# The long convolution's layer norm and its product, by halves of tokens

## What is computed

```python
def layernorm(x, g, b):
    mu = jnp.mean(xf, axis=-1, keepdims=True)
    var = jnp.mean(jnp.square(xf - mu), axis=-1, keepdims=True)
    y = (xf - mu) * lax.rsqrt(var + EPS)
    return (y * g + b).astype(x.dtype)

def conformer_conv(x, norm_g, pw1_w, pw1_b, dw_w, dw_b, ln_g, ln_b, pw2_w, pw2_b):
    a, b = jnp.split(rmsnorm(x, norm_g) @ pw1_w + pw1_b, 2, axis=-1)
    h = a * jax.nn.sigmoid(b)
    h = <causal convolution of width 31, each channel by itself>(h, dw_w) + dw_b
    h = jax.nn.silu(layernorm(h, ln_g, ln_b))
    return h @ pw2_w + pw2_b
...
        h = h + conformer_conv(h, ...)
        h = h + swiglu_ffn(h, ffn_norm[layer], ffn_w_in[layer], ffn_w_out[layer])
```

## Time and profile before

| | us |
|---|---|
| median of 3 runs | 1077.83 |
| lowest, highest | 1077.32, 1078.03 |
| the profiled execution, its own time | 1077.06 |
| its span in the trace | 1075.3 |
| TensorE busy | 1032.3 |
| VectorE busy | 700.5 |
| ScalarE busy | 531.0 |

### The profile page before, as it was taken

One profiled execution on the slowest core, in us unless ns is written; L12 is line 12 of the kernel. 1 busy time (PEld: TensorE's weight loads), 2 busy tenths in 40 slices (PEclk: granted clock), 3 DMA queues, 4 the chain that ended last, 5 costly groups with the idle time before them and its releaser, 6 DMA issues.

```text
span 1075.3 us, 15964 instructions
## 1 busy us (share of the span) xinstructions
PE 1032.3 (96%) x6529; PEld 888.0 (83%) x6529; DVE 700.5 (65%) x1085; ACT 531.0 (49%) x809; POOL 79.4 (7%) x125
## 2 busy tenths in 40 slices
PE   6997999999999989999999999999899999999997
PEld 6984788888889846888888889988678889998996
DVE  3997566666668587666766668848665456555554
ACT  5424455545554477654455464436465445434442
POOL 2000093000001011000000011000000000000000
PEclk9998999999999989999999999999999999999999
DMA  8873546667555501756676546644234435565530
GB/s 226 235 211 101 154 137 202 173 204 206 178 118 180 180 1 38 218 157 196 178 210 200 169 148 226 192 158 158 79 126 150 156 118 189 164 200 191 180 134 40
DMA packets 188995, 174.21 MB, mean 162 GB/s; under 512 B 12822, under 2 KB 164502, under 8 KB 188922
## 3 DMA queue, kind: packets, MB, share of 16 engines
q1 hardware_dynamic: 187216, 169.67, 51.8%
q10 hardware_dynamic: 1322, 2.62, 0.8%
q0 software_dynamic: 384, 0.90, 0.2%
HBM read 171.24 MB, written 1.93 MB: 161 GB/s over the span
## 4 chain that ended last, share of the span: by engine, by line
PE 79%; DVE 12%; ACT 4%; DMA 2%; issue 2%; POOL 0%; SPq 0%; POOLq 0%; ACTq 0%; DVEq 0%
PE bank L1866 17%; PE bank L1867 16%; PE bank L1868 16%; PE bank L1951 11%; PE bank L1950 6%; DVE split_lo L1115 4%; PE bank L2093 2%; ACT split_hi L675 2%; PE bank L1947 2%; DVE xn L1132 1%; DMA v<-in_ml_conv_w 1%; PE bank L2258 1%; PE bank L1903 1%; PE bank L1948 1%; DVE v L1572 1%
## 5 line engine op out<-in xcount | busy, mean ns | idle before, releaser
L1115 DVE TENSOR_TENSOR split_lo<-raw,split_hi 128x2048 fp32r<-128x2048 f32 (+1 forms) x157 | 354.6, 2273 | 146.3 <-ACT split_hi L675 145.9
L675 ACT ACTIVATE split_hi<-raw 128x2048 fp32r<-128x2048 f32 (+1 forms) x157 | 295.2, 1893 | 84.5 <-PE bank L1868 77.4
L1866 PE MATMUL bank<-xn,split_hi 128*128 128x256 f32 (+1 forms) x752 | 215.7, 287 | 5.3 <-DVE xn L1132 4.6
L1951 PE MATMUL bank<-xn,split_hi 128*128 128x512 f32 x616 | 219.8, 396 | 0.0
L1867 PE MATMUL bank<-xn,split_hi 128*128 128x256 f32 (+1 forms) x752 | 212.6, 283 | 0.0
L1868 PE MATMUL bank<-xn,split_lo 128*128 128x256 f32 (+1 forms) x752 | 212.5, 283 | 0.0
L1950 PE MATMUL bank<-xn,split_lo 128*128 128x256 f32 x616 | 172.2, 280 | 0.5 <-DVE xn L1132 0.5
L1866 PEld LDWEIGHTS bank<-xn,split_hi 128*128 128x128 f32 (+1 forms) x752 | 143.0, 190 | 10.4 <-issue 4.4
L1867 PEld LDWEIGHTS bank<-xn,split_hi 128*128 128x128 f32 (+1 forms) x752 | 143.1, 190 | 0.7
L1868 PEld LDWEIGHTS bank<-xn,split_lo 128*128 128x128 f32 (+1 forms) x752 | 143.1, 190 | 0.0
L1951 PEld LDWEIGHTS bank<-xn,split_hi 128*128 128x128 f32 x616 | 115.6, 188 | 23.7
(11 more groups left out here) (322 smaller groups left out, 1203.4 us busy)
## 6 DMA issues: line engine op xcount, KB each, us to landing
raw<-in_ffn_w_in SPq DMA_DIRECT2D x88, 512.0 KB, 5.2
raw<-in_w_ff SPq DMA_DIRECT2D x32, 1024.0 KB, 5.3
raw<-in_ffn_w_out SPq DMA_DIRECT2D x22, 1024.0 KB, 5.0
raw<-in_w_in SPq DMA_DIRECT2D x14, 1024.0 KB, 5.3
raw<-in_a_pw_w SPq DMA_DIRECT2D x16, 512.0 KB, 7.9
raw<-in_w_xkv SPq DMA_DIRECT2D x8, 1024.0 KB, 5.4
raw<-in_a_pw_w SPq DMA_DIRECT2D x4, 1024.0 KB, 9.0
raw<-in_b_w_in SPq DMA_DIRECT2D x4, 1024.0 KB, 6.0
```

Of the source, the lines that this page charges most:

```text
L675: nc.scalar.activation(split_slot[m % SPLITS][0][:, 0:n], raw[c % RAWS][:, 0:n], ACT.Copy).then_inc(split_hi, 1)
L1115: return nc.vector.tensor_tensor(dst, src, hi.bitcast(F32), ALU.subtract)
L1866: mm(dst, left[0], right[0], start=start, stop=False)
L1951: x = mm(whole, hi, xn_both[:, :, kt, :], start=False, stop=kt == KT - 1)
```

## The change

- The last convolved tile (7) is computed in two halves of tokens into two banks (5 and 6), evacuated and squared by halves. In place of five sums of tiles on TensorE there are one over a tile that VectorE has summed (tiles 0, 1, 5 and 6, in `tile_sum`) and two of 128 columns for tile 7; in place of four sums of squares there are one for tile 4 (before the last convolution), one over what VectorE has summed, and two of 128 columns for tile 7. So "last tiles in a row" are tile 7's halves, and the order of squaring becomes tiles 2 to 4, 0 and 1, 5 and 6, 7.
- The square of the offset goes to ScalarE. The load of the Sqrt table goes ahead of the evacuation of tile 5.
- Reciprocal, centring, normalising, SiLU and splitting are done for the first 128 tokens of all tiles and then for the other 128. ScalarE makes the high part (`ACT.Copy`); VectorE only the low one.
- The first column half of the product runs over token halves outside and channel halves inside, so it holds two chunks at a time.
- The bias row is no product any more: it is loaded over all 128 partitions (512 KB in place of 4) and added to `h` by VectorE, in two instructions of 128x1024 between the last SiLU tile and the split of `pw2[2]`.

```diff
-        SQUARES = [slice(2, 5), slice(5, 7), slice(0, 2), slice(7, 8)]
+        SQUARES = [slice(2, 5), slice(0, 2), slice(5, 7), slice(7, 8)]
+        tile_sum = softf[:, 0:S]
+        LAST_BANK = [5, 6]
+        NORMED = [[1, 2, 3, 3, 4, 4, 5, 5], [6, 6, 7, 7, 8, 8, 9, 9]]
...
-                sc.dma_start(pw2_row, a["a_pw2_b"]).then_inc(small_loaded, 16)
+                sc.dma_start(gain_row[:, :], a["a_pw2_b"].broadcast_to([P, D])).then_inc(bias_loaded, 16)
...
+            nc.scalar.activation(msq[:, 18:19], eps_col[:, :], ACT.Sqrt)
             conv_evac(3)
+            square_about_pivot(0)
             conv_evac(4)
-            square_about_pivot(0)
             square_about_pivot(1)
             square_about_pivot(2)
-            conv_evac(5)
-            square_about_pivot(3)
-            nc.scalar.activation(msq[:, 18:19], eps_col[:, :], ACT.Sqrt)
+            for t in range(TT):
+                sc.wait_ge(quad_done, 6 + t)
+                nc.scalar.activation(v[:, 7, tok(t)], bank[LAST_BANK[t]][:, tok(t)], ACT.Identity,
+                                     bias=vecT[:, col["a_dw_b"] + 7:col["a_dw_b"] + 8]).then_inc(conv_out, 1)
+            for t in range(TT):
+                sc.wait_ge(centred, 4 + t)
+                part = u[:, 7, PAD + P * t:PAD + P * t + P]
+                nc.scalar.activation(part, part, ACT.Square).then_inc(squared, 1)
+            sc.wait_ge(offset_ready, 1)
+            nc.scalar.activation(offset, offset, ACT.Square).then_inc(offset_squared, 1)
...
+            for t in range(TT):
+                for ft in range(KT):
...
+                    sc.wait_ge(normed, NORMED[t][ft])
+                    nc.scalar.activation(v[:, ft, tok(t)], v[:, ft, tok(t)], ACT.Silu,
...
+                    if first or ft % 2:
+                        part = (slice(None), slice(ft if first else ft - 1, ft + 1), tok(t))
+                        sc.wait_ge(silu_ready, n + 1)
+                        nc.scalar.activation(xn[0][part], v[part], ACT.Copy).then_inc(silu_hi, 1)
...
             for g in range(4):
-                silu_halves(g)
+                silu_low(g, 0)
                 if g + 2 < 4:
-                    centre(g + 2)
-                    normalise(g + 2)
+                    centre(g + 2, 0)
+                    normalise(g + 2, 0)
+                if g == 2:
+                    inverse(1)
+                    centre(0, 1)
+                    normalise(0, 1)
+            centre(1, 1)
+            normalise(1, 1)
+            for g in range(4):
+                silu_low(g, 1)
+                if g + 2 < 4:
+                    centre(g + 2, 1)
+                    normalise(g + 2, 1)
+            ve.wait_ge(bias_loaded, 16)
+            for t in range(TT):
+                nc.vector.tensor_tensor(h[:, t, :], h[:, t, :], gain_row[:, :], ALU.add).then_inc(bias_added, 1)
             through(chunk_of["pw2"][2])
...
+                parts = [weights("pw2", 0, 4)]
+                for t in range(TT):
+                    for half in range(2):
...
+                        c, w = parts[half]
+                        for q in range(4):
+                            kt = 4 * half + q
+                            te.wait_ge(silu_lo, NORMED[t][kt])
+                            x = mm3(bank[acc_bank(FFN0, t, 0)][:, :], part(xn, ALL, kt, tok(t)), part(w, ALL, q, ALL),
+                                    kt == 0, kt == KT - 1)
```

190 lines of the change are left out of this document (110 added, 80 removed).

## The result

| | before | after |
|---|---|---|
| median of 4 runs each, on one chip | 1077.74 | 1070.76 |
| lowest, highest | 1077.32, 1078.03 | 1068.90, 1071.45 |
| the profiled execution, its own time | 1077.06 | 1068.90 |
| its span in the trace | 1075.3 | 1067.0 |

The ratio is 0.9934, with a 95% interval of 0.992 to 0.9947: the change makes the kernel 7.0 us faster, between 5.7 and 8.6 us. Repeated beside another set of runs it was 1071.87 against 1077.78, 5.9 us, a ratio of 0.9945 (0.9927 to 0.9963). The forecast was 1071.8 and the range 1069.2 to 1075.2. The first median lies just under the forecast's own part of that range (1070.8 to 1073.0), the second inside it.

A forecast was written before the change was run, and what follows sets the result against it. TensorE, 96% busy, bounds the kernel, its longest wait a 5.5 us chain ahead of `pw2`. Split of `pw2[2]` at 111.5 plus 12.0 gives 123.5 instead of 129.54: 1077.83 - 6.0 = 1071.8, range 1069.2 to 1075.2.

The forecast's parts named there:

- just there: Last convolution's start: its rows' last load has landed by 85.62, in time for a start at 85.75.
- The nearest row: Last convolution: measured 64-column pieces at 0.034 us each, taken for the 128 pieces of 128 columns, 4.35 us.
- a late convolution: Rival at the last convolution: late rows or pieces at 0.056 cost 2 us, giving 1073.8; chance 0.09.
- The statistics, the root and the first tile: Ahead of the product: variance closed at 92.95, 1.3 us sooner; first SiLU 95.0; first product 96.2 against 99.95.
- neither bound: Tiles' end, forecast 106.9: 104.9 if VectorE never waits, 108.5 if a 128-token SiLU costs as much as 256.
- The cover of 6.5 us: Split of `pw2[2]` before: ended 108.8, wanted 115.3; now forecast to end at 111.5, TensorE waiting 1.2 us.
- TensorE bound instead of the split: Rival in the product: tiles end at 104.9 or the clock stays up; gain 7.3 to 8.5 us, 1069.3 to 1070.8; chance 0.19.
- the second fall: Rival: the clock falls again behind the wait for `pw2[2]`, costing 1.7 to 3 us, 1073.5 to 1075; chance 0.12.
- a sign of being wrong: Wrong if the `pw2[2]` wait is missing or over 3 us, clock differs, or later stages aren't all 6 us earlier.
- a clock that stays low: Slower rival in the product: each us low costs 0.47, gain gone past 118.9, up to 1087 us; chance 0.04.
- The bias row's term: Four bias products of 1.05 us leave TensorE, three of them on the path: 3.2 us.
- given back: Rival behind the stretch: longer waits in the attention layers eat the gain, within 2 us of before; chance 0.06.

The follow-up runs named there:

- e9: The changed kernel with ScalarE issuing the bias row's broadcast load later, behind the squares of tiles 5 and 6; median 1070.84 us, ratio 0.9946 to the kernel before.
- e10: The changed kernel with the late bias row load and VectorE splitting `pw2[2]` before adding the bias row; median 1068.59 us, ratio 0.9928 to the kernel before.
- e12: The changed kernel with late load, nine unread products in TensorE's wait, and `pw2[2]` split ahead of tile 7's squares; 1068.10 us, ratio 0.9919 to before.
- e7: The changed kernel with nine additional unread products in TensorE's wait ahead of the product; median 1071.80 us, ratio 0.9943 to the kernel before.
- e8: The changed kernel with nine unread products in TensorE's wait and `pw2[2]` split before the bias row is added; 1068.89 us, ratio 0.9915 to before.
- e6: The changed kernel with VectorE splitting `pw2[2]` before it adds the bias row; median 1069.69 us, ratio 0.9930 to the kernel before.
- e5: The changed kernel run again unaltered, beside another set of runs; median 1071.87 us, ratio 0.9945 to the kernel before.
- e1: The kernel before with only the bias row loaded over all partitions and added by VectorE ahead of the `pw2[2]` split; 1073.00 us, ratio 0.9956.
- e11: The changed kernel with late load, `pw2[2]` split before the bias row, and nine unread products in TensorE's wait; 1068.88 us, ratio 0.9921 to before.

## Why the prediction was right

Its times lean on `conv(4)` ending at 85.3. In the changed kernel's trace that is 84.29, so 1.02 is added to each mark here.

| | predicted | measured + 1.02 |
|---|---|---|
| the last convolution starts | 85.75 | 86.64 |
| its pieces | 4.35 for 128 | 3.63 |
| the variance is closed | 92.95 | 93.20 |
| first SiLU | 95.0 | 95.17 |
| first product; the wait ahead of it | 96.2; 4.3 | 96.47; 4.18 |
| clock back | 102.1 | 101.6 |
| last low part | 106.9 | 107.1 |
| TensorE wants `pw2[2]` | 110.0 to 110.4 | 110.04 |
| its split ends | 111.5 | 111.57 |
| wait for it | 1.2 | 1.59 |
| the second half | 12.0 | 11.93 |
| the feed-forward network's first product | 123.5 | 123.56 |

**The last convolution** is where two terms were wrong and cancelled. Its rows were not "just there": it started 1.33 us behind the end of `conv(4)`, 0.70 of that in a wait, where the prediction had 0.45. With the load of the bias row later it is 0.57 in e9, but 0.73 in e10 and 0.70 in e12, and with the early load 0.72 and 0.70 in e7 and e8; so the load is a likely cause and not a shown one. Part of it belongs to the one sum, which took 0.57 and not 0.45 even without a wait. And the pieces of 128 columns did not cost 0.034 but 3.63 / 128 = 0.028. The nearest row, 64 columns at 0.034, was no guide: halving the width from 256 (0.056) halved the cost. Here the measurement goes with the Trainium skill ("TensorE: Matmul & The Clock Gate", section LDWEIGHTS): its rule, columns over 1.2 GHz, makes an estimate of 27 ns for the weight load of 32 columns, just under the 28 ns that a piece took. The prediction had set it aside for the row. Had both terms been right, the sum would have been nearly the same; that they cancelled is luck. The rival of a late convolution thus did occur, at 0.9 us instead of 2, and was paid for by the pieces.

**The statistics, the root and the first tile** came within 0.3 us. The table load was what came last, and the reciprocal of half the tokens took the 0.95 us estimated, the SiLU 0.49.

**The tiles.** ScalarE and VectorE take turns as worked out. In the second token half VectorE waits for ScalarE's copy by 0.27, 0.17 and 0.80 us, the last low part's start comes at 105.66, and neither bound (104.9, 108.5) was near.

**The bias row and the new wait.** VectorE needed 2.35 + 2.28 us behind the last low part, as the sum had it. The cover of 6.5 us was gone, and the split of `pw2[2]` became what TensorE waits for. e6 shows it as the cause. The wait is 0.4 longer than predicted, by the sum chiefly because the clock came back 0.8 us sooner behind the product's start (0.4 us at 0.47 each), which TensorE could use for nothing else: the rival "TensorE bound instead of the split" names the same thing, that an unfallen clock would only lengthen this wait, and e7 shows it (2.60 us) along with the second fall, at some 1.6 us. In the change itself the second fall did not come.

**The clock** took another course than forecast, which the prediction had named as a sign of being wrong. It was to fall about 1.2 us into the wait and be back 5.9 us after the product's start; it fell 2.5 us in and was back after 5.1, and in e5, the same kernel, it fell only 0.7 us after the product had begun and was back 4.1 us after its start. The time did not feel it, since VectorE's split set the end of the first half: the stretch is 36.92 and 36.91 us. Had TensorE been what bound, this would have been an error of 0.4 us in the one and 1.2 in the other. Two smaller readings were off: the low stretch behind 763 lasts 3.6 us in the trace of before (from 764.4 to 768.0) and not 3.2, and by the rival's own terms (6.0 and 1.2 us at 0.47 each) a clock that stays low eats the gain from about 117.5 on, not 118.9.

**The bias row's term** of 3.2 us on the path was too small, at 3.75 (e1). The forecast did not go by it: the 12.0 us of the second half were built from products, and are right.

**Behind the stretch** nothing was given back: the distance is 7.0 us at 129.54, 165.55, 316.54 and 340.54 of the trace before, and only the two falls of the clock in the attention layers add to it. By medians the gain is 7.0 and 5.9 us in two sets of runs, and 6.0 was the sum.

The first median, 1070.76, could as well be claimed by the rival "TensorE bound instead of the split" (1069.3 to 1070.8); it is the wait of 1.59 us and e6 that decide for the forecast's mechanism, and not the time.

What the prediction lacked is a question rather than a number. It costed the bias row's place, saw that it takes the cover, and did not ask what the place was for; two lines exchanged are worth 2 us.

## What to carry to other kernels

When work moves from the engine that bounds the kernel to another, look at what that engine has queued behind it. Work that is needed last belongs last in the queue: here additions that were worth 3 to 4 us alone were worth 0.8 beside the token halves (some 1.9 at a like clock), ahead of a split of weights, and 2 us came back by putting them behind it.

A wait is only worth shortening up to the next one: work out for each edit when TensorE arrives at its next operand and when that operand is ready, and keep both times. Half the tokens started the product 2.07 us sooner and, with the split late, finished it 0.40 us sooner, with the split first 2.35; full clock in the first half gained nothing for the same reason.

Questions of 1 us in a kernel of 1070 are better put to a stretch between two marks of the trace than to medians of whole runs. But one trace is one execution: what varies from one to the next, as the clock and the landing of rows do here, needs several.

## What the runs showed of the hardware that I had not expected

- The granted clock takes different courses in the same program. In two executions of the change it fell at about 93.75 and at about 96.3, the second time only after the product had begun, and was back at about 100.55 and 99.8. Waits of 1.59 and 2.35 us inside the product were followed by no fall, one of 2.60 us (e7) by one that began 1.4 us after the wait was over.
- Matrix products of 32 by 128 columns that share the array cost 0.028 us each, 32 by 256 columns 0.056, but 32 by 64 columns 0.034, more than those twice as wide.
- A load of 512 KB over all partitions landed after 6.1 us when issued at 71.3, that is at 77.4, about when tile 7's rows were stored at 77.28; yet those rows mostly came some 1 us later than without it. Transfers that had been pushed back behind it would explain that; no run here tells. In the eight traces with the early load it took 4.4 to 6.2 us, and in the four with the late one, issued at 85.9 in e9, 6.9 to 7.5, with nothing disturbed that TensorE waited for.
- The landing of a 143 KB store and its loads back can slip: in e11 it left TensorE waiting 2.08 us, and with the fall of the clock behind it and a start 1 us later put the whole execution 5 us back.
